# Three pairs of hidden chunks per gated layer as seven block products, with larger weight sums formed by accumulating loads

## What is computed

```python
def swiglu(h, wg, wu, wd):
    return (jax.nn.silu(h @ wg) * (h @ wu)) @ wd

h = rmsnorm(x, g[0])
x = x + 0.5 * rmsnorm(swiglu(h, ffn_wg[l, 0], ffn_wu[l, 0], ffn_wd[l, 0]), g[1])
```

## Time and profile before

| | |
|---|---|
| median of 3 runs | 1484.91 us (1483.28 to 1486.76) |
| the profiled execution | 1485.87 us |
| its span, first to last instruction | 1484.1 us |
| PE busy | 1383.7 us, 93% |
| VectorE (DVE) busy | 1101.7 us, 74% |
| ScalarE (ACT) busy | 819.8 us, 55% |
| moved by DMA | 274.37 MB, mean 185 GB/s |

### The profile page before, as it was taken

How to read it: one execution, slowest core, us unless ns; L and a number is a source line. 1 busy time by engine, 2 the same in 40 slices (tenths; PEclk the granted TensorE clock), 3 DMA queues, 4 the chain that set the end, 5 groups by cost and what they waited for, 6 DMA issues and landing times. The chain is left out here.

```text
span 1484.1 us, 19388 instructions
## 1 busy us (share of the span) xinstructions
PE 1383.7 (93%) x6943; PEld 1145.2 (77%) x6943; DVE 1101.7 (74%) x1565; ACT 819.8 (55%) x1301; POOL 80.3 (5%) x133
## 2 busy tenths in 40 slices
PE   5999999999995999999895999987999999959998
PEld 4878877999974888887674888866888877848886
DVE  6577786989778887479969887579785546698863
ACT  4547746655545555366655555455464567655552
POOL 3011100000000000031100000000000100000000
PEclk8999999999997999999997999997999999989999
DMA  9887654676542747353262847426575473438460
GB/s 353 287 285 232 216 170 146 209 272 230 198 156 85 255 129 266 120 184 114 86 213 85 257 144 252 150 92 224 172 236 189 126 221 115 156 100 269 143 226 29
DMA packets 160702, 274.37 MB, mean 185 GB/s; under 512 B 5953, under 2 KB 87617, under 8 KB 160609
## 3 DMA queue, kind: packets, MB, share of 16 engines
q1 hardware_dynamic: 153904, 250.86, 50.7%
q0 software_dynamic: 5552, 20.20, 4.4%
q10 hardware_dynamic: 1153, 2.07, 0.4%
HBM read 272.05 MB, written 1.06 MB: 184 GB/s over the span
## 5 line engine op out<-in xcount | busy, mean ns | idle before, releaser
L2327 DVE TENSOR_TENSOR w_lo<-raw,w_hi 128x1024 fp32r<-128x1024 f32 (+1 forms) x312 | 370.8, 1231 | 78.4 <-ACT w_hi L2065 77.5
L2065 ACT ACTIVATE w_hi<-raw 128x1024 fp32r<-128x1024 f32 (+1 forms) x312 | 309.8, 1047 | 102.6 <-PE psum L2801 54.4
L2799 PE MATMUL psum<-w_hi,hT_hi 128*128 128x512 f32 x760 | 307.1, 404 | 6.3 <-DVE hT_lo L2493 3.7
L2800 PE MATMUL psum<-w_lo,hT_hi 128*128 128x512 f32 x760 | 298.0, 392 | 0.0
L2801 PE MATMUL psum<-w_hi,hT_lo 128*128 128x512 f32 x760 | 297.9, 392 | 0.0
L2799 PEld LDWEIGHTS psum<-w_hi,hT_hi 128*128 128x128 f32 x760 | 144.2, 190 | 40.5 <-issue 10.0
L2801 PEld LDWEIGHTS psum<-w_hi,hT_lo 128*128 128x128 f32 x760 | 144.2, 190 | 31.2
L2800 PEld LDWEIGHTS psum<-w_lo,hT_hi 128*128 128x128 f32 x760 | 144.5, 190 | 27.8 <-issue 0.6
L2799 PE MATMUL psum<-w_hi,hc_hi 128*128 128x512 f32 x256 | 101.2, 395 | 0.7 <-DVE hc_lo L2718 0.6
L2801 PE MATMUL psum<-w_hi,hc_lo 128*128 128x512 f32 x256 | 99.9, 390 | 0.0
L2800 PE MATMUL psum<-w_lo,hc_hi 128*128 128x512 f32 x256 | 99.8, 390 | 0.0
(11 more groups left out here) (301 smaller groups left out, 2831.8 us busy)
## 6 DMA issues: line engine op xcount, KB each, us to landing
raw<-in_ffn_wd_dram SPq DMA_DIRECT2D x44, 1024.0 KB, 5.0
raw<-in_ffn_wg_dram SPq DMA_DIRECT2D x56, 512.0 KB, 4.0
raw<-in_ffn_wu_dram SPq DMA_DIRECT2D x56, 512.0 KB, 5.3
raw<-in_w_up_dram SPq DMA_DIRECT2D x44, 512.0 KB, 5.1
raw<-in_w_in_dram SPq DMA_DIRECT2D x19, 1024.0 KB, 7.7
raw<-in_ffn_wg_dram SPq DMA_DIRECT2D x16, 1024.0 KB, 5.2
raw<-in_ffn_wu_dram SPq DMA_DIRECT2D x16, 1024.0 KB, 5.2
ada_raw<-in_w_ada_dram POOLq DMA_DIRECT2D x24, 512.0 KB, 5.4
```

The source lines that it names most:

```text
L2065: nc.scalar.activation(hi_of(s)[:, cs], source_of(s)[:, cs], ACT.Copy).then_inc(ready, 1)
L2327: nc.vector.tensor_tensor(lo_of(u)[:, cs], source_of(u)[:, cs], hi_of(u)[:, cs].bitcast(F32), ALU.subtract)\
L2799: nc.tensor.matmul(o, a_hi, b_hi, start=start, stop=False)
L2800: nc.tensor.matmul(o, a_hi, b_lo, start=False, stop=False)
```

## The change

`GROUPS` becomes (2, 5, 8): three pairs per gated layer, with a single chunk (4 and 7) between two pairs and the tail (10) right after the third. The block products use another set of combinations, so that u6 and u4 are `blended` plus a weight block that comes straight from memory. These two sums are no longer formed by VectorE: GpSimd issues a DMA of 1 MB that adds the block into `blended` as it lands (`accum_op`). It issues u6's once u5 is split, and u4's once u6 is split; ScalarE's splits of u6 and u4 wait for the whole of it. u5 and u7 are still formed by VectorE, with additions. u2 is loaded by SyncE right after u7 and is now fourth: u1, u5, u7, u2, u6, the down unit, u3, u4. ScalarE's activation of the first token tile follows u2 at once, and its product on VectorE moves into `gup`. The mixed tokens are prepared in `go_on`: VectorE's six instructions ahead of the first up products of the second token tile in the list, ScalarE's hi part after `out(0)`, VectorE's lo part after the split of the first down unit and ahead of the first `hidden_turn`.

```diff
@@ -48,7 +48,7 @@
 FIRST = 4
-GROUPS = (2, 6)
+GROUPS = (2, 5, 8)
 MORE = 3 * len(GROUPS)
@@ -159,8 +160,14 @@
         u = self.unit(4, BANK, [(0, BANK, load)] if load is not None else [])
-        a, b = (u if v == "own" else v for v in (a, b))
-        self.formed[u] = dict(no=len(self.formed), dst=dst, a=a, b=b, last=self.last_sum if dst == "sums" else None)
+        a, b = (u if isinstance(v, str) and v == "own" else v for v in (a, b))
+        last = self.last_sum if dst == "sums" else None
+        if isinstance(b, int):
+            self.formed[u] = dict(by="vector", no=self.n_formed, dst=dst, a=a, b=b, last=last)
+            self.n_formed += 1
+        else:
+            self.formed[u] = dict(by="dma", no=self.n_landed, dst=dst, src=b, last=last)
+            self.n_landed += 1
         if dst == "sums":
@@ -871,11 +878,17 @@
         def go_on(self):
             us = [u for c in (0, 1) for u, _ in self.units[c]]
             if not self.conv:
+                pl.add("token_rows", g=self.G[KT - 1, 1])
                 self.st = x_stats(x_at)
+                pl.add("token_sums")
             self.mm(0, 1)
             self.mm(1, 1)
             self.out(0)
+            if not self.conv:
+                pl.add("token_high")
             pl.split_to(us[3] + 1)
+            if not self.conv:
+                pl.add("token_low")
             self.mm(2, 1)
             self.hidden_turn(0)
             pl.split_to(us[3] + 2)
@@ -887,9 +900,7 @@
                 return
-            pl.add("mixed_rows", g=self.G[KT - 1, 1])
             self.down(0)
-            pl.add("mixed_split")
             self.hidden_turn(1)
@@ -925,18 +936,23 @@
                 pl.split_ahead(u)
                 pl.add("gprod", unit=u, use=use, start=start, **of)
...
+            banks = (4, 5, 6, 7) if c % 2 == 0 else (6, 7, 4, 5)
             u1 = pl.unit(4, BANK, [(0, BANK, block(gate, 0))])
             u5 = pl.sum_unit(block(up, 0), "sums", "own", u1)
-            u7 = pl.sum_unit(block(up, 4), u5, "own", u5)
-            u6 = pl.sum_unit(None, "sums", u7, "sums")
+            u7 = pl.sum_unit(block(up, 4), u5, u5, "own")
+            u2 = pl.unit(4, BANK, [(0, BANK, block(gate, 4))])
+            u6 = pl.sum_unit(None, "sums", "sums", block(up, 4))
             pl.release[u1], pl.release[u5] = u5, u7
-            banks = (4, 5, 6, 7) if c % 2 == 0 else (6, 7, 4, 5)
-            p1, p5, p7, p6 = (pl.use(b, u) for b, u in zip(banks, (u1, u5, u7, u6)))
+            p1, p5, p7 = (pl.use(b, u) for b, u in zip(banks, (u1, u5, u7)))
             product_of(u1, p1, True, tile=(0, 0), mixed=None)
             product_of(u5, p5, True, tile=None, mixed=3)
             pl.add("gkeep", use=p1, slot=0)
             product_of(u7, p7, True, tile=None, mixed=2)
             pl.add("gkeep", use=p5, slot=1)
+            p2 = pl.use(banks[0], u2)
+            product_of(u2, p2, False, tile=(4, 0), mixed=None)
+            pl.add("ggate", t=0, use=p2, stat=self.st, n=n)
+            p6 = pl.use(banks[3], u6)
             product_of(u6, p6, True, tile=None, mixed=0)
             pl.add("gsum", kept=(p1, p5), uses=(p6, p7), n=n)
             self.down(c - 1)
@@ -944,13 +960,8 @@
             p3 = pl.use(banks[1], u3)
             product_of(u3, p3, False, tile=None, mixed=1)
-            pl.add("gup", use=p3, n=n)
-            u2 = pl.unit(4, BANK, [(0, BANK, block(gate, 4))])
-            p2 = pl.use(banks[0], u2)
-            product_of(u2, p2, False, tile=(4, 0), mixed=None)
-            pl.add("ggate", t=0, use=p2, stat=self.st, n=n)
-            u4 = pl.sum_unit(None, "sums", u2, "sums")
-            pl.release[u2] = u4
+            pl.add("gup", use=p3, gate=p2, stat=self.st, n=n)
+            u4 = pl.sum_unit(None, "sums", "sums", block(gate, 4))
             p4 = pl.use(banks[2], u4)
             product_of(u4, p4, False, tile=(4, 1), mixed=None)
@@ -1947,6 +1958,13 @@
                     load_half(0, 0)
                     load_half(0, 1)
+                elif kind == "split_hi":
+                    made = plan.formed.get(a["unit"])
+                    if made is not None and made["by"] == "dma":
+                        pool.wait_ge(hi_ready, made["last"] + 1)
+                        pool.wait_ge(lo_ready, made["last"] + 1)
+                        pool.dma_start(blended.rearrange("p (k n) -> p k n", k=4), made["src"], accum_op=ALU.add)\
+                            .then_inc(sum_landed, 16)
                 elif kind == "ada" and a["own"] is not None:
                     if a["own"] + 1 < len(plan.ada_own):
@@ -2060,8 +2078,10 @@
                     cs = half_of(s, half)
-                    if made is not None:
+                    if made is not None and made["by"] == "vector":
                         act.wait_ge(sum_ready, 2 * made["no"] + half + 1)
+                    elif made is not None:
+                        act.wait_ge(sum_landed, 16 * (made["no"] + 1))
                     nc.scalar.activation(hi_of(s)[:, cs], source_of(s)[:, cs], ACT.Copy).then_inc(ready, 1)
@@ -2222,7 +2242,7 @@
                                                  scale=col(a["stat"], "r", t)).then_inc(silu_ready, 1)
-                elif kind == "mixed_rows":
+                elif kind == "token_high":
                     n_mixed[0] += 1
@@ -2300,23 +2320,22 @@
-                if u not in plan.formed or u in formed:
+                if u not in plan.formed or u in formed or plan.formed[u]["by"] == "dma":
                     return
...
                 for v in (made["a"], made["b"]):
-                    if v != "sums" and v not in plan.formed or v == u:
+                    if v != "sums" and (v not in plan.formed or v == u or ("w", v) in raw_slot):
                         dve.wait_ge(weight_loaded[raw_slot["w", v]], landed["w", v])
-                if made["dst"] == "sums":
-                    if made["last"] is not None:
-                        dve.wait_ge(hi_ready, made["last"] + 1)
-                        dve.wait_ge(lo_ready, made["last"] + 1)
+                if made["last"] is not None:
+                    dve.wait_ge(hi_ready, made["last"] + 1)
+                    dve.wait_ge(lo_ready, made["last"] + 1)
                 if made["no"]:
                     dve.wait_ge(sum_ready, 2 * made["no"])
-                plus, minus = raw_of(made["a"]), blended if made["b"] == "sums" else raw_of(made["b"])
+                a, b = (blended if v == "sums" else raw_of(v) for v in (made["a"], made["b"]))
                 for half in range(2):
                     cs = half_of(u, half)
-                    nc.vector.tensor_tensor(source_of(u)[:, cs], plus[:, cs], minus[:, cs], ALU.subtract).then_inc(sum_ready, 1)
+                    nc.vector.tensor_tensor(source_of(u)[:, cs], a[:, cs], b[:, cs], ALU.add).then_inc(sum_ready, 1)
@@ -2355,9 +2374,7 @@
-                elif kind == "mixed_rows":
-
-
+                elif kind == "token_rows":
@@ -2365,17 +2382,18 @@
                     n_mixed[0] += 1
+                elif kind == "token_sums":
                     base = 6 * n_mixed[0] - 6
...
                     dve.wait_ge(tokens_mixed, base + 2)
-                    nc.vector.tensor_tensor(x22, x21, x22, ALU.add).then_inc(tokens_mixed, 1)
+                    nc.vector.tensor_tensor(x22, x22, x21, ALU.subtract).then_inc(tokens_mixed, 1)
                     dve.wait_ge(tokens_mixed, base + 3)
...
                     dve.wait_ge(tokens_mixed, base + 4)
-                    nc.vector.tensor_tensor(x11, x22, x11, ALU.subtract).then_inc(tokens_mixed, 1)
+                    nc.vector.tensor_tensor(x11, x22, x11, ALU.add).then_inc(tokens_mixed, 1)
                     dve.wait_ge(tokens_mixed, base + 5)
-                    nc.vector.tensor_tensor(x12, x12, x11, ALU.subtract).then_inc(tokens_mixed, 1)
-                elif kind == "mixed_split":
+                    nc.vector.tensor_tensor(x12, x11, x12, ALU.subtract).then_inc(tokens_mixed, 1)
+                elif kind == "token_low":
                     dve.wait_ge(tokens_hi_ready, n_mixed[0])
@@ -2383,35 +2401,30 @@
                     wait_ready(dve, p7)
-                    nc.vector.tensor_tensor(kept[:, 1, :], psum[:, p7.bank, :], kept[:, 1, :], ALU.add)\
-                        .then_inc(psum_read[p7.bank], 1)
+                    nc.vector.tensor_tensor(kept[:, 1, :], psum[:, p7.bank, :], kept[:, 1, :], ALU.add).then_inc(psum_read[p7.bank], 1)
                     wait_read(dve, p1)
                     wait_ready(dve, p6)
-                    nc.vector.tensor_tensor(kept[:, 0, :], psum[:, p6.bank, :], kept[:, 0, :], ALU.add)\
-                        .then_inc(psum_read[p6.bank], 1)
+                    nc.vector.tensor_tensor(kept[:, 0, :], kept[:, 0, :], psum[:, p6.bank, :], ALU.subtract).then_inc(psum_read[p6.bank], 1)
                     wait_read(dve, p6)
                     wait_read(dve, p7)
```

(32 more changed lines are left out.)

6 lines of the change are left out of this document (5 added, 1 removed).

## The result

| | time, us | ratio to before | 95% interval |
|---|---|---|---|
| before | 1485.56 (1483.28 to 1486.76) | 1 | |
| after | 1572.77 (1571.73 to 1576.73) | 1.0594 | 1.057 to 1.0617 |

The change makes the kernel 5.9% slower, 87 us. The forecast was 1510, in a range of 1466 to 1542: the sign was right and the time lies above the range.

The account below looks back on a forecast made before the run. TensorE was taken as the bound, VectorE next. Per layer -1.0 (tokens) - 2.7 (third pair) + 7.0 (group turns) + 3.2 (tail) = +6.5, four layers +26: 1485.87 + 26 - 1 = 1511, said as 1510 us, range 1466 to 1542.

Parts of the forecast that it names:

- Part 1: Mixed tokens prepared sooner in each gated layer: a gain of 1.0 us per layer, from +2.3 to a loss of 4.
- the new stall: TensorE waits 4.1 us for the hidden lo part at the end of chunk 1's up products.
- ends u7 at 473.2: First layer: TensorE starts the first mixed product at about 467.8 and ends u7's product at 473.2.
- the stall behind gkeep: u2 waits about ten us for product 1's bank, freed by ScalarE's gkeep behind hi u6; u2 starts at 483.
- Part 2: The third pair saves one block product of eight, 12 matmuls, 2.7 us per layer on TensorE.
- Part 3: Accumulating loads: 6.7 us from issue to landing, 7.0 from the end of the split that releases them.
- Rival (c): Accumulating DMA is slow: landing after 10 us adds 7.8 us per layer, 1541 us; 20%, together with the falling clock.
- Part 4: Order within and after a pair: VectorE's later chain adds stalls of 7.0 us per layer, plus 3.2 in the tail.
- about 0.6: After a pair, gup is done at t = 25.5, which holds chunk c+2 for about 0.6 us.
- the group turn 3.5: After chunks 4 and 7, TensorE waits 3.5 us for the second group_turn's lo part, ready 41.0, wanted 37.5.
- The clock, counted at nothing: Four new stalls of 3 to 4 us per layer may let the clock fall; nothing was counted for it.
- The forecast's own bound, 38 us: Upper limit for low clock behind the new stalls: at most 2.4 us each, 38 us in all.

Follow-up runs that it names:

- after_mended: Changed kernel with token hi/lo parts after the first hidden turn, later splits behind the second, and u3's low split behind gup; 1586.13 us, ratio 1.0679.
- after_plain: Changed kernel with the same GpSimd DMAs as plain copies, the addition left out, so u6 and u4 are plain weight blocks; 1519.91 us, ratio 1.0238.
- after_vsum: Changed kernel with u6 and u4 summed by VectorE from the raw blocks of u7 and u2, no accumulating DMA; 1529.78 us, ratio 1.0305.
- third_pair_only: Kernel before with pairs at 2, 5 and 8 and nothing else; 1490.53 us, ratio 1.0042.
- the new order: New unit order and combinations: changed kernel with VectorE's sums, 1529.78 us, against the kernel before with early tokens and third pair, 1477.29 us.
- the mended order: Changed kernel with VectorE's sums, tokens split after the first hidden turn, later splits behind the second, u3's low split behind gup; two pairs: 1474.05 us.
- vsum_free7: Changed kernel with VectorE's sums, u3 reading u2's raw block so u7's slot is free once u6 is split; 1512.03 us, ratio 1.0181.

## Why the prediction was right or wrong

**Part 1, the tokens.** Right in its places: the low part of the tokens was to end at 458.3 and the new stall to take 4.1 us; they ended at 459.0 and took 4.2. Wrong at "ends u7 at 473.2": the forecast gave u7 its weights and forgot its bank. That bank waits for the second hidden turn, 5.3 us at the first pair and 23.8 in all. In the changed kernel this cost nothing by itself, since u2 would have waited anyway: the stall behind gkeep is the shorter for it (3.0 in the mean, not 10), and where the bank was free in time (after_mended) that stall is 13.8 in the mean. So the chain that the forecast wrote down, gkeep behind u6's split behind u6's load, was the right one. Its own rule ("if it has landed by 478.3 ... u2 starts at 483") with the measured landing, 483.1, gives 487.8; u2 started at 487.5. Chunk 4 began at 510.4, not 502.4: of these 8 us, 4.5 are u6's late load by way of gkeep, and 3 are the bank that gup frees (3.5 in place of 0.6). The sum also had a slip: with its own landing, 6.7 to 7.0 us from 468.9, ScalarE's list sets the pace and u2 starts at 481.7, not 483, 1.3 us per layer or 5 in all.

**Part 2.** The 2.7 us per layer are confirmed (9.5 us for 48 matmuls, against 11). But its cost on VectorE was only counted where group_turn needs it; alone it is 16.5 to 25 us once the long stall is gone.

**Part 3, the step that failed most.** "From issue to landing I take 6.7 us"; it was 11.2, in the median 13.4 for u6 and 8.6 for u4. With plain copies, landing after 7.0, the same kernel took 1519.9, near the sum of 1510. In part that is luck: the stall of ten us behind gkeep is not there (one of 5.8 for the third product's bank stands in its place), 20.4 us are waits for the bank that gup frees, and the clock was counted at nothing. Rival (c) named the slow landing and priced it at 31 us for 10 us of landing; it cost 43 to 53. What its price left out is TensorE's clock. Between the profiled executions of after_plain and of the changed kernel, 47 us apart, idle time makes up 25 us; the other 23 are busy time for the same matmuls (1421.9 against 1399.0).

SyncE's loads beside the accumulating ones slow down too (9.0 from 5.0), but that they cost anything is not shown. ScalarE's waits for weight loads, summed over all lines, are 226 us in the changed kernel, of which 113.5 are for the accumulating loads and 112.5 for SyncE's; in after_vsum, with no accumulating load at all, those for SyncE's are 172.5. For the down weights, the loads that slowed, ScalarE waited 20.2 us, against 17.1 in after_vsum.
The Trainium skill, "Collectives: The Full Stack", section "The bandwidth ceiling: the fold count and why AG ≠ RS ≠ AR", has a DMA that adds at half the rate, in collectives of several ranks, since it reads two sources. The direction is borne out: 11.2 against 7.0 for the same bytes on the same queue, a factor of 1.6 and not 2. The reason is not tested here.

**Part 4.** The forecast gave gup "about 0.6" and the group turn 3.5. It was the other way round in the changed kernel: about 3.5 us (up to 3.7) at the up unit behind each of the twelve pairs, and almost nothing at the group turn (2.2 us in 4 waits), since TensorE had already stood still. VectorE at the second pair shows it; TensorE had ended u4 at 562.9, and went on at 566.38, once gup had read the bank:

```profile
561.04 4.63 DVE L2346 TENSOR_TENSOR w_lo<-raw,w_hi 128x1024 fp32r<-128x1024 f32 x4
565.59 0.69 DVE L2414 SCALAR_TENSOR_TENSOR gate_rows<-psum,gate_rows 128x512 f32<-128x512 f32 x1
```

Four halves of low splits stand ahead of gup, and one product (2.73 us) covers them where there were two. In after_plain the forecast's wait is there, 20.8 us in 9 waits for the group turn, besides 20.4 for the bank.

**The clock, counted at nothing.** third_pair_only and the changed kernel run the same 6895 matmuls: busy for 1374.2 and 1421.9 us, idle for 112.0 and 148.2. So 48 of the 84 us between them are busy time, and most of that is matmuls at a lower clock: in the stretches whose granted clock is at the low level TensorE was busy for 36 us in the one and 117 us in the other. At half the speed half of it is lost, 18 and 58 us, which accounts for some 40 of the 48 (an estimate). Busy time and granted clock of the changed kernel by stretch (columns as in the earlier trace rows), and the thirteenth matmul behind the stall of 4.2 us:

```profile
459.00:466.00 7.00, 6.11 (x16) 4.84 (x17) 7.00 (x9) 2.12 (x2) 0.00 (x0) 0.55 0.36 137
466.00:479.00 13.00, 8.06 (x38) 6.32 (x36) 8.43 (x9) 4.62 (x5) 1.33 (x1) 1.00 0.65 181
...
484.00:487.50 3.50, 0.00 (x0) 0.00 (x0) 3.25 (x3) 3.50 (x6) 0.33 (x1) 0.75 0.01 2
487.50:492.00 4.50, 4.47 (x11) 3.51 (x12) 3.66 (x4) 2.35 (x3) 0.97 (x1) 0.50 0.65 97
```
```profile
465.15 0.46 PE L2812 MATMUL psum<-hi_qk,hc_hi 128*128 128x512 f32 x1
```

Behind the stall of 4.2 us the clock is at its low level (1.2 of 2.4 GHz) for some 5 us, and twelve matmuls take 5.3 (459.89 to 465.15) in place of 2.73. The stall of 15.7 us before cost 2.4 in the same way: this short stall pays as much as the long one. Others pay less: behind the 3.5 us ahead of 566.38 twelve matmuls take 4.1. The forecast's own bound, 38 us, was nearer than the zero in its sum.
The Trainium skill, "TensorE: Matmul & The Clock Gate", section "HAM oscillation — how this bites in real kernels", warned of gaps between bursts; the trace agrees, with a gap of 4.2 us.

**What stays open.** Of the 52.5 us of the new order, the slot explains 18. The bank behind gkeep shows as 24.6 us of waits at two pairs in the mended order, but was not tried alone; that the rest, and the 72 us of the third pair there, come from a list of VectorE that runs late is argued from waits, not shown. A fourth raw slot would tell more; it wasn't tried.

## What to carry to other kernels

Taking a sum from an engine that is not the bound, and giving it to a transfer, replaces work that is hidden by latency that isn't: price the landing, the queue beside it and the slots before the engine time saved. When a unit is moved forward in a ring of few slots, ask for every unit behind it what it still holds and for which bank its product waits. Several short stalls in place of a long one cost more than their own length: TensorE's busy time at the low clock was 36 us in third_pair_only, which has the long ones, and 117 in the changed kernel. Count the clock behind each stall.

## What the runs showed of the hardware

- An accumulating load of 1 MB from DRAM into SBUF landed after 11.2 us (8.3 to 13.8), a plain copy of it on the same queue after 7.0 (5.4 to 10.5); issuing it took GpSimd 1.28 us against 0.75, and 24 of them added 6,144 packets.
- Plain loads of the down weights on SyncE's queue took 9.0 us in the median beside accumulating loads, against 6.9 beside plain copies and 5.0 in the kernel before. Not all of this is the neighbour: in vsum_free7, with neither kind on GpSimd's queue, they took 6.8, so when they are issued counts too.
- With a quarter of its bytes the accumulating load landed after 6.3 and 4.1 us, and the kernel was 57 us faster.
- A stall of 4.2 us brought TensorE's clock to its low level, and cost another 2.5 us of slow matmuls behind it, as the one of 15.7 us had (2.4); one of 3.5 us cost another 1.4.
